# Inverse norms changed between row and token form through device memory instead of TensorE products, in a two-layer decoder trunk

## The reference, cut to what matters

```python
def rmsnorm(x, g):
    return x * lax.rsqrt(jnp.mean(x * x, axis=-1, keepdims=True) + EPS) * g

for i in range(DEPTH):                                   # DEPTH = 2
    x = x + 0.5 * swiglu_ffn(rmsnorm(x, n_ffn1[i]), ...)
    h = rmsnorm(x, n_mix[i])
    mix = gla_mixer(h, ...) if i % 2 == 0 else pool_mixer(h, ...)
    x = x + mix
    x = x + mem_cross_attn(rmsnorm(x, n_xattn[i]), rmsnorm(mem, n_mem[i]), ...)
    x = x + 0.5 * swiglu_ffn(rmsnorm(x, n_ffn2[i]), ...)
return rmsnorm(x, n_final)

def gla_mixer(h, ...):                                   # the lines that matter here
    q, k, v, r = jnp.split(h @ w_in, ...)
    glog = jax.nn.log_sigmoid((h @ w_g1) @ w_g2 + b_g) / GATE_TAU

def pool_mixer(h, w_grp, b_grp, scale):
    for gi, w in enumerate((2, 4, 8, 16)):               # a quarter of the features each
        u = h[..., gi * 256:(gi + 1) * 256]
        groups.append(causal_window_mean(u, w) - u)
    # each group times its own 256x256 matrix, plus b_grp, times scale
```

## Time and profile before

| what | us |
|---|---|
| median of 3 runs (lowest, highest) | 2011.03 (2009.01, 2011.12) |
| the profiled execution | 2009.44 |
| its span in the trace | 2007.5 |
| PE busy | 1999.6 |
| DVE busy | 927.6 |
| ACT busy | 706.6 |
| POOL busy | 99.7 |

### The profile page before, as it was taken

One profiled execution on the slowest core, in us unless ns is written; L12 is line 12 of the kernel. 1 busy time (PEld: TensorE's weight loads), 2 busy tenths in 40 slices (PEclk: granted clock), 3 DMA queues, 4 the chain that ended last, 5 costly groups with the idle time before them and its releaser, 6 DMA issues.

```text
span 2007.5 us, 23376 instructions
## 1 busy us (share of the span) xinstructions
PE 1999.6 (100%) x9344; PEld 1671.2 (83%) x9344; DVE 927.6 (46%) x995; ACT 706.6 (35%) x852; POOL 99.7 (5%) x109
## 2 busy tenths in 40 slices
PE   9999999999999999999999999999999999999999
PEld 7888888888898888888888888888898888888887
DVE  5343343577765544334243443433276544333334
ACT  5222232356553443222222322232156443222222
POOL 2000001000010020000001000000002010000000
PEclk9999999999999999999999999999999999999999
DMA  5322252212333332332323323222343123223231
GB/s 174 105 95 93 99 142 92 86 63 84 112 120 105 105 106 88 101 104 84 100 94 99 105 84 104 93 90 94 99 147 109 60 84 105 98 90 104 89 106 58
DMA packets 196393, 199.32 MB, mean 99 GB/s; under 512 B 12034, under 2 KB 188288, under 8 KB 196336
## 3 DMA queue, kind: packets, MB, share of 16 engines
q1 hardware_dynamic: 186192, 193.21, 29.6%
q0 software_dynamic: 1360, 3.47, 0.6%
q10 hardware_dynamic: 8784, 1.84, 0.5%
HBM read 195.36 MB, written 3.15 MB: 99 GB/s over the span
## 4 chain that ended last, share of the span: by engine, by line
PE 97%; DVE 1%; ACT 1%; issue 0%; DMA 0%; ACTq 0%; DVEq 0%
PE ps L337 32%; PE ps L338 32%; PE ps L339 32%; PE ps L886 0%; DVE w_lo L1633 0%; PE ps L674 0%; ACT w_hi L1116 0%; PE ps L849 0%; PE ps L622 0%; DMA x_tok<-in_x 0%; DVE v_lo L1636 0%; PE ps L1030 0%; PE ps L1031 0%; PE ps L1108 0%; PE ps L983 0%
## 5 line engine op out<-in xcount | busy, mean ns | idle before, releaser
L337 PE MATMUL ps<-h_hi,w_hi 128*128 128x512 f32 (+1 forms) x1728 | 667.2, 386 | 1.4 <-DVE gate_odd L1919 1.4
L338 PE MATMUL ps<-h_lo,w_hi 128*128 128x512 f32 (+1 forms) x1728 | 665.6, 385 | 0.0
L339 PE MATMUL ps<-h_hi,w_lo 128*128 128x512 f32 (+1 forms) x1728 | 665.6, 385 | 0.0
L1633 DVE TENSOR_TENSOR w_lo<-raw,w_hi 128x2048 fp32r<-128x2048 f32 (+4 forms) x195 | 417.6, 2142 | 458.7 <-ACT w_hi L1116 458.4
L1116 ACT ACTIVATE w_hi<-raw 128x2048 fp32r<-128x2048 f32 (+4 forms) x195 | 347.5, 1783 | 249.4 <-PE ps L339 246.6
L337 PEld LDWEIGHTS ps<-h_hi,w_hi 128*128 128x128 f32 x1728 | 324.6, 188 | 66.6 <-DVE w_lo L1633 1.9
L339 PEld LDWEIGHTS ps<-h_hi,w_lo 128*128 128x128 f32 x1728 | 324.6, 188 | 64.6
L338 PEld LDWEIGHTS ps<-h_lo,w_hi 128*128 128x128 f32 x1728 | 324.7, 188 | 64.2
L337 PE MATMUL ps<-mid_hi,w_hi 128*128 128x512 f32 (+1 forms) x710 | 275.1, 387 | 0.0
L338 PE MATMUL ps<-mid_lo,w_hi 128*128 128x512 f32 (+1 forms) x710 | 274.9, 387 | 0.0
L339 PE MATMUL ps<-mid_hi,w_lo 128*128 128x512 f32 (+1 forms) x710 | 274.9, 387 | 0.0
(11 more groups left out here) (335 smaller groups left out, 1603.1 us busy)
## 6 DMA issues: line engine op xcount, KB each, us to landing
raw<-in_ffn_w_gu SPq DMA_DIRECT2D x87, 1024.0 KB, 5.1
raw<-in_ffn_w_down SPq DMA_DIRECT2D x32, 1024.0 KB, 5.1
raw<-in_x_w_kv SPq DMA_DIRECT2D x16, 1024.0 KB, 5.6
raw<-in_ffn_w_down SPq DMA_DIRECT2D x16, 768.0 KB, 4.4
raw<-in_gla_w_in SPq DMA_DIRECT2D x12, 1024.0 KB, 5.1
raw<-in_x_w_q SPq DMA_DIRECT2D x8, 1024.0 KB, 5.1
raw<-in_x_w_o SPq DMA_DIRECT2D x8, 1024.0 KB, 5.1
raw<-in_gla_w_out SPq DMA_DIRECT2D x8, 512.0 KB, 3.4
```

Source lines behind the costliest of these rows:

```text
L337: nc.tensor.matmul(out_ap, left[0], right[0], start=first, stop=False)
L338: nc.tensor.matmul(out_ap, left[0], right[1], start=False, stop=False)
L339: return nc.tensor.matmul(out_ap, left[1], right[0], start=False, stop=last)
L1633: return nc.vector.tensor_tensor(out_ap, value, hi.bitcast(F32), ALU.subtract)
```

## The change

It adds a small tensor in device memory, `rms_scratch` (2 x 4 x 128 floats), and three semaphores. For the gated norm, `norm(1)` makes the row form only; POOL stores row 0 of `rms` to the scratch, waits, and loads it back as `rms_tok`, and ACT and DVE wait for `tok_loaded` ahead of `values`. For the pooling norm, PE's four matmuls and the DVE copy of `spread_rms(5)` are gone; POOL stores `rms_tok` to the scratch, waits, loads it as a row to all 128 partitions of `rms`, and DVE waits for `rms_loaded` ahead of the `up` operations (L2308). Two waits of PE for PSUM banks 5 and 4 go with the readers of these banks.

```diff
+        rms_scratch = nc.dram_tensor("rms_scratch", [2, T, P], F32).ap()
...
-        RMS_FEEDS = (0, 1, 3, 4, 5, 7)
+        RMS_FEEDS = (0, 1, 3, 4, 7)
         SUM_FEEDS = (1, 3, 4, 7)
-        SPREAD_FEEDS = (0, 5)
-        TOK_FEEDS = (0, 1, 2, 5, 6, LAST)
+        SPREAD_FEEDS = (0,)
+        TOK_FEEDS = (0, 2, 5, 6, LAST)
...
+            pool.wait_ge(sig.norm_ready, RMS_FEEDS.index(1) + 1)
+            pool.dma_start(rms_scratch[0:1].rearrange("o t p -> o (t p)"), rms[0:1, :]).then_inc(sig.rms_stored, 16)
+            pool.wait_ge(sig.rms_stored, 16)
+            pool.dma_start(rms_tok[:], rms_scratch[0].rearrange("t p -> p t"), allow_slow_non_contiguous=True)\
+                .then_inc(sig.tok_loaded, 16)
+
             pool.wait_ge(sig.mem_stored, MT * 4 * 16)
...
             bands()
             add_squares(5)
+            pool.wait_ge(sig.tok_ready, TOK_FEEDS.index(5) + 1)
+            pool.dma_start(rms_scratch[1].rearrange("t p -> p t"), rms_tok[:], allow_slow_non_contiguous=True)\
+                .then_inc(sig.rms_stored, 16)
+            pool.wait_ge(sig.rms_stored, 32)
+            pool.dma_start(rms[:], rms_scratch[1:2].rearrange("o t p -> o (t p)").broadcast_to([P, SEQ]))\
+                .then_inc(sig.rms_loaded, 16)
...
                 pe.wait_ge(sig.norm_ready, 2)
-                pe.wait_ge(sig.tok_ready, TOK_FEEDS.index(1) + 1)
...
-                if m == 5:
-                    pe.wait_ge(sig.norm_ready, RMS_FEEDS.index(5) + 1)
...
             cross_keys(1, (1,))
-            spread_rms(5)
             transpose_tokens(2)
...
             def values(pair):
+                act.wait_ge(sig.tok_loaded, 16)
...
             def values(pair, tiles):
+                dve.wait_ge(sig.tok_loaded, 16)
...
             cross_keys(1, (1,))
-            spread_rms(5)
             tokens(2)
             tokens(3)
+            dve.wait_ge(sig.rms_loaded, 16)
             dve.wait_ge(sig.counts_ready, 7)
```

More of the change, by code:

```diff
@@ L297, in trunk @@
                 band_step band_hi_ready band_lo_ready xt_transposed xt_hi_ready xt_lo_ready
-                band_done pt_hi_ready pt_lo_ready half_taken half_done half_x half_sq first_w_hi first_w_lo x_in_act x_in_dve tok_squared t1_taken"""
+                band_done pt_hi_ready pt_lo_ready half_taken half_done half_x half_sq rms_stored tok_loaded rms_loaded first_w_hi first_w_lo x_in_act x_in_dve tok_squared t1_taken"""
         sig = namedtuple("Semaphores", names)(*[sem(name) for name in names.split()])
```

## The result

| | before | changed |
|---|---|---|
| median (lowest, highest), us | 2010.09 (2009.01, 2011.12), 6 runs | 2017.92 (2017.64, 2019.97), 6 runs |
| the profiled execution, its span | 2009.44, 2007.5 | 2017.64, 2015.7 |

The ratio is 1.0041, with an interval of 1.0032 to 1.0051: the change makes the kernel slower by some 8 us. The forecast of 2009.5 us was wrong and so was its range. Rival 2, to which I gave 0.08, holds the measured time.

What follows compares the result with a forecast made beforehand. PE's instruction stream, busy 1999.6 of 2007.5 us, was taken as the kernel's length. Gains of 0.81 us (gated) and 0.72 us (pooling) sum to 1.53 us, from 2011.03 to 2009.5 us; range 2007.4 to 2013.0.

Steps and rivals of the forecast that it cites:

- Rival 2: POOL's scattered store or load in the pooling mixer is very slow, making the kernel over 4.0 us slower; chance 0.08.
- the store's term: POOL's store of 512 separate floats in the pooling mixer: taken as 3.3 us, between 2.3 and 5.2 us.
- The load: POOL's load of 256 KB to 128 partitions in the pooling mixer, mostly between two weight transfers: 3.5 us.
- The mechanism: Pooling mixer: row form late by d delays `up` and PE by d, so the time grows one for one.
- The sign that the prediction named: DVE idle ahead of `up`, ended by a DMA, proves it wrong; that idle time less 1.5 us is the slowdown.
- The gated half: Gated norm: PE loses four one-column matmuls, 0.81 us gained; the wait for `tok_loaded` costs nothing, the 1.4 us stall stays.
- The pooling half's gain: Pooling mixer: the missing DVE copy gives 0.72 us if the row form is in SBUF when DVE wants it.
- rival 3: The full PE time comes back, 0.89 us in the pooling mixer, 2.0 us in all, 2009.0 us; chance 0.10.
- rival 1: Pooling row form a little late: load held by DVE's `w_lo` split, or DMAs near high ends; 2010.5 to 2013.1; chance 0.25.

Runs made afterwards that it cites:

- the probe: The kernel before with extra DMAs of various shapes in POOL's idle time, data unused; first set 2011.06 us, second set 2041 us, one run each.
- the run without the store: The changed kernel without the pooling half's store, loading the gated half's row instead (wrong values); 2007.66 us, ratio 0.999.
- The version with whole pieces: The changed kernel storing the pooling norm as 128 pieces of 16 bytes, the `up` operations reading `rms` with a step of four; 2010.09 us, ratio 0.9999.
- the gated half alone: The changed kernel with the pooling half undone, its norm spread on TensorE as before; 2008.47, 2008.74 and 2008.26 us, ratios 0.9993, 0.9997, 0.9994.
- the way round: The changed kernel with the pooling norm's four columns sent to a row in SBUF, then to device memory as one piece; 2014.0 us, ratio 1.0022.

## Why the prediction was wrong, point by point

**The step that failed** is the store's term: "Between: 3.3 us for the 64 KB of gate weights, which are 1024 pieces of 64 bytes on POOL's queue, twice as many pieces as here. I take 3.3 us, by the number and smallness of the pieces." It took 11.4 us, over twice my upper bound of 5.2: 4.3 us until its last packet had gone behind the weight transfer, and 7.2 us from there until it had landed. The row I leaned on is a load, and this is a store; the pieces of that row are 64 bytes, and 512 stored pieces of 64 bytes take 2.2 us in the probe, so the row said nothing wrong about them. Neither number nor smallness alone makes the time. What does is that pieces of 4 bytes are written next to each other in device memory, and none of the rows that bounded the store did that. The same bytes in pieces of 16 took 5.0 us, so the neighbours cost 6.4 us, and the other 1.7 us over my 3.3 are the weight transfer beside the store, which I had seen and put at nothing. The upper bound, a DMA in a queue of others, was the slowest row I had and not a bound for this operation. I wrote that no row spoke against rival 2, and gave it 0.08.

**The load** was put at 3.5 us and took 5.9. The 2.4 us follow from the same step. The prediction had the load between two weight transfers. The 1 MB weight that SP sends some 7.5 us behind the first one usually lands after 5.0 us (before, and in the run without the store). In the changed kernel the DMA view gives for this one

```profile
raw<-in_x_w_kv SPq DMA_DIRECT2D x1, 1024.0 KB, 9.9
```

and the stretches of the changed kernel (length, then busy us of PE, PEld, DVE, ACT and POOL, the clock, the DMA engines' share and GB/s) show when it was moved:

```profile
1474.00:1478.00 4.00, 4.00 (x35) 4.00 (x35) 3.57 (x3) 1.94 (x4) 0.00 (x0) 1.00 0.00 0
1478.00:1482.00 4.00, 4.00 (x35) 3.91 (x34) 0.05 (x1) 3.15 (x4) 0.55 (x1) 1.00 0.27 35
...
1484.00:1486.00 2.00, 2.00 (x19) 2.00 (x18) 0.00 (x0) 0.00 (x0) 0.00 (x0) 1.00 1.08 408
```

against the version without the store:

```profile
1478.00:1482.00 4.00, 4.00 (x35) 3.91 (x34) 3.97 (x7) 3.29 (x4) 0.00 (x0) 1.00 0.68 253
```

From 1474 to 1478 us no packet ran at all, and the store, whose packets were through, had still not landed. The weight sent at 1476.75 then barely moved, 35 GB/s where it has 253 otherwise, and came at 408 GB/s after the store had landed, on top of the load. So the slow store held up what was sent after it, and pushed the weight into the load's time. What was sent before it was not held up: the weight of 1469.28, 0.36 us ahead of the store, landed after 5.1 us. With SP as the sender the store left 0.4 us ahead of that weight, and the weight took 13.8 us, the next one 11.4 and the load 7.4.

**The mechanism was right.** "Late by d ... the time grows by d, one for one": `up` starts 21.96 us after the first transpose instead of 13.33, 8.63 us later; PE's matmul comes 8.64 us later. The sign that the prediction named came too: DVE's idle time ahead of `up`, 9.26 us, less 1.5 is 7.8 us. The version with the step in `rms` fits as well: `up` 0.24 us earlier, 1.65 us longer, PE 1.42 us later (1465.25 to 1518.62, 53.37 us). And rival 2 had the price right: "16 to 20 us for the pair" gave 2016.9 to 2020.9 us; the pair took 17.6 us, the time 2017.92.

**The gated half** was put at 0.81 us and is worth 0.86 to 0.93 in the traces (by medians 1.1 to 1.4). The stall of 1.4 us stayed, no wait for `tok_loaded` appears, both as said. **The pooling half's gain** was put at 0.72 us and is 0.71 where the data are there in time; the full 0.89 us of PE (rival 3) did not come back. **Sum:** 8.64 - 0.86 = 7.8 us slower by the stages, 7.8 by the medians (2017.92 - 2010.09).

**The first half of rival 1**, a load held up by DVE's split, could not show in the changed kernel, where DVE was idle when the load left at 1481.36. The version with whole pieces has the case: its load left at 1474.78, under this split, and between 1475.9 and 1476.5 us, ahead of the split's end at 1476.62, 17 of its packets ran. DVE's row and POOL's queue:

```profile
1474.33 2.29 DVE L1643 TENSOR_TENSOR w_lo<-raw,w_hi 128x2048 fp32r<-128x2048 f32 x1 [1.31 <-ACT w_hi L1125]
```

```profile
q0 software_dynamic: 17, 0.07, 47.5%
```

The split did not hold the load, as the prediction had read from the earlier trace rows.

Of the versions that compute the whole, the gated half alone is the fastest, 1.1 to 1.4 us under before by its medians, which these runs can't tell from none with certainty.

## What to carry to other kernels

A transpose by DMA costs by what it does to the side that is written: let the scattered side be the one that is read, and the written side whole rows or pieces of 16 bytes and more, or at least pieces that start 16 bytes or more apart. Bound an operation only with rows that do the same thing in the same direction; where no row does, the slowest row of the page is not an upper end, and the mechanism that nothing speaks against deserves more than a few per cent. Put a small DMA that something waits for where no 1 MB transfer is under way, or count 2 to 3 us more for it, and send nothing urgent behind a slow store.

## What the runs showed of the hardware that was not expected

**Neighbouring stores of 4 bytes** take 9 to 11 us for 512 of them and 7 to 9 us for 128, against 2.2 us when they start 16 to 64 bytes apart with no weight transfer ahead of them. Their packets are gone after 1.3 to 1.9 us where nothing is in the way; the rest is waiting for the landing. A 1 MB transfer sent meanwhile takes 10 to 14 us instead of 5 (12.4 and 12.9 us beside the probes).

**A small DMA of POOL's behind a weight transfer of SP's** doesn't mix with it: sent 0.4 us behind the weight, the packets of the store, of the load without the store and of the four columns all stand at or behind 1473.2 us, when the weight's last ones run.

**PE's clock falls after a wait of 4 us.** PE waited 4.08 us for `w_lo` ahead of 1493.09. Its timeline from there:

```profile
1493.09 0.79 PE L338 MATMUL ps<-w_hi,h_hi 128*128 128x512 f32 x1 [4.08 <-DVE w_lo L1643]
1493.68 0.63 PE L339 MATMUL ps<-w_lo,h_hi 128*128 128x512 f32 x1
1494.11 0.63 PE L340 MATMUL ps<-w_hi,h_lo 128*128 128x512 f32 x1
...
1499.23 0.42 PE L340 MATMUL ps<-w_hi,h_lo 128*128 128x512 f32 x1
1499.48 0.39 PE L338 MATMUL ps<-w_hi,h_hi 128*128 128x512 f32 x1
```

The stretches (the clock is the third number from the end):

```profile
1493.09:1499.23 6.14, 6.14 (x14) 4.79 (x15) 4.91 (x8) 3.27 (x4) 0.00 (x0) 0.50 0.55 173
1500.00:1510.00 10.00, 8.59 (x37) 6.47 (x36) 9.86 (x11) 5.70 (x6) 0.00 (x0) 1.00 0.35 107
```

For 6 us the matmuls follow each other every 0.43 us instead of 0.23, and are 0.63 us long instead of 0.39: the granted clock of the stretch is 0.50, the lower of the two levels, 1.2 instead of 2.4 GHz, and then 1.00 again. The same happened behind the 3.67 us wait of the way round (its stretch from 1498.80 to 1505.00 us has a granted clock of 0.72) and behind one of 3.70 us with the store on SP's queue, for 3.5 and 4.8 us; it did not happen behind waits of 1.4 and 1.5 us. In these 6.14 us PE ran 14 matmuls, which take some 3.2 us at the upper level, so 2.9 us went there; that is most of why PE is busy 2002.0 us, against 1997.7 us in the version without the store, which has the same instructions on PE. Against that version the pooling half is 9.35 us longer (60.59 and 51.24 us): 5.5 us are waits, 2.9 us the clock, and the rest short gaps next to the waits. But the clock is not a cost of its own here: PE waited again for DVE at 1502.51 (0.80 us) and at 1508.85 (0.61 us), so the slow matmuls ran in time that PE would have waited for anyway. From the start of `up` to PE's matmul it is 38.63 us, and 38.62 us before. In a place where PE sets the pace it should come on top; no run here shows that.
